# A transformer block and a mixture-of-experts block on one core: where the feed-forward stage starts, and in which order its last down products are made

## The reference, cut to what matters

```
def swiglu(x, w_gate, w_up, w_down):
    return (jax.nn.silu(x @ w_gate) * (x @ w_up)) @ w_down

# first block, around the change
f = swiglu(rms_norm(h, ffn1_norm_pre), ffn1_w_gate, ffn1_w_up, ffn1_w_down)
h = h + 0.5 * rms_norm(f, ffn1_norm_post)
u = rms_norm(h, mix_norm_pre)
proj = u @ w_in                 # queries, keys, values, recurrence, gates
...
f = swiglu(rms_norm(h, ffn2_norm_pre), ffn2_w_gate, ffn2_w_up, ffn2_w_down)
h = h + 0.5 * rms_norm(f, ffn2_norm_post)

# second block: the modulation, computed from c and w_ada
mod = jax.nn.silu(c) @ w_ada + b_ada
```

## Time and profile before

| | |
|---|---|
| time, median of 3 runs | 2217.12 us (2217.07 to 2219.19) |
| profiled execution, its own time | 2215.6 us |
| its span | 2213.7 us, granted clock 0.99 |
| PE busy | 2145.5 us, 97% |
| PEld busy | 1317.0 us, 59% |
| DVE busy | 853.4 us, 39% |
| ACT busy | 379.9 us, 17% |
| moved by the DMA engines | 581.61 MB, mean 263 GB/s |

### The profile page before, as it was taken

The page is one execution under the profiler, slowest core; times in us unless marked ns, Lnnn a source line. Parts: engine busy times, 40 slices in busy tenths (PEclk is TensorE's granted clock), DMA queues, the critical chain, the costliest instruction groups (busy, mean ns, idle before and its releaser), DMA issues.

```text
span 2213.7 us, 33878 instructions
## 1 busy us (share of the span) xinstructions
PE 2145.5 (97%) x14809; PEld 1317.0 (59%) x14810; DVE 853.4 (39%) x1400; ACT 379.9 (17%) x812; POOL 92.6 (4%) x106
## 2 busy tenths in 40 slices
PE   8999999999999999999998999999999999999997
PEld 6667687888677765678887533444444444344432
DVE  2667386621344444367777511112211121111113
ACT  1001200240111122344333110001100110000000
POOL 1000000000000011122121000000000000000000
PEclk9999999999999999999999899999999999999999
DMA  8697766244535460000012699999999999999996
GB/s 302 217 317 238 264 237 209 86 143 153 199 115 171 155 226 10 3 3 3 23 51 98 266 383 426 424 427 425 425 425 427 425 425 423 419 423 426 426 426 268
DMA packets 153876, 581.61 MB, mean 263 GB/s; under 512 B 9556, under 2 KB 108700, under 8 KB 120704
## 3 DMA queue, kind: packets, MB, share of 16 engines
q1 hardware_dynamic: 149744, 564.70, 64.9%
q0 software_dynamic: 3568, 12.72, 1.7%
q10 hardware_dynamic: 416, 2.01, 0.3%
HBM read 578.32 MB, written 3.43 MB: 263 GB/s over the span
## 4 chain that ended last, share of the span: by engine, by line
PE 90%; DVE 5%; DMA 2%; issue 1%; ACT 1%; SPq 1%; DVEq 0%
PE ps L2876 23%; PE ps L728 11%; PE ps L2884 10%; PE ps L919 8%; PE ps L796 7%; PE ps L1636 4%; PE ps L2855 3%; PE ps L2917 3%; PE ps L1079 2%; PE ps L1012 2%; PE ps L1965 2%; PE ps L1985 2%; PE ps L2067 1%; PE ps L1253 1%; DMA arena<-in_w 1%; PE ps L1982 1%
## 5 line engine op out<-in xcount | busy, mean ns | idle before, releaser
L2876 PE MATMUL ps<-ring,const 128*64 128x512 f32 (+1 forms) x1536 | 473.9, 596 | 0.0
L2876 PEld LDWEIGHTS ps<-ring,const 128*64 128x64 f32 (+1 forms) x1536 | 160.6, 144 | 304.8 <-issue 304.5
L2876 PE MATMUL ps<-arena,const 128*64 128x512 f32 (+1 forms) x512 | 225.7, 593 | 0.0
L3115 DVE TENSOR_SCALAR arena<-ps 128x1024 f32<-128x1024 f32 x18 | 22.0, 1225 | 469.3 <-PE ps L2876 469.3
L2884 PE MATMUL ps<-ring,const 128*64 128x512 f32 (+1 forms) x768 | 190.4, 594 | 1.0 <-DMA ring<-in_w 1.0
L728 PE MATMUL ps<-ring,arena 128*128 128x256 f32 x800 | 185.0, 382 | 4.6 <-DMA ring<-in_ffn_w_down 4.4
L919 PE MATMUL ps<-arena,ring 128*128 128x256 f32 x800 | 173.0, 379 | 0.0
L728 PEld LDWEIGHTS ps<-ring,arena 128*128 128x128 f32 x800 | 151.2, 191 | 26.4 <-issue 4.4
L919 PEld LDWEIGHTS ps<-arena,ring 128*128 128x128 f32 x800 | 152.0, 190 | 20.9
L796 PE MATMUL ps<-ring,arena 128*128 128x512 f32 x352 | 154.7, 592 | 0.0
L2884 PEld LDWEIGHTS ps<-ring,const 128*64 128x64 f32 (+1 forms) x768 | 65.6, 143 | 112.4 <-issue 110.9
(11 more groups left out here) (517 smaller groups left out, 2604.0 us busy)
## 6 DMA issues: line engine op xcount, KB each, us to landing
ring<-in_w SPq DMA_DIRECT2D x96, 2048.0 KB, 19.4
ring<-in_w SPq DMA_DIRECT2D x96, 1024.0 KB, 17.2
arena<-in_w SPq DMA_DIRECT2D x32, 2048.0 KB, 20.1
ring<-in_w_in SPq DMA_DIRECT2D x26, 1536.0 KB, 7.3
arena<-in_w SPq DMA_DIRECT2D x32, 1024.0 KB, 19.2
ring<-in_w_ada SPq DMA_DIRECT2D x16, 1536.0 KB, 7.7
ring<-in_ffn_w_gate SPq DMA_DIRECT2D x44, 512.0 KB, 4.9
ring<-in_ffn_w_up SPq DMA_DIRECT2D x44, 512.0 KB, 6.1
```

What stands on the lines that cost most here:

```text
L2876: ins = pe.matmul(ps[a * n:(a + 1) * n, q, :], xsT[:, k, a * n:(a + 1) * n], chunk(chunks[a])[:, q * 512:(q + 1) * 512], start=False, stop ...
```

## The change

Five edits. Ten products of the identity with itself go to PSUM bank 6, which nobody reads before it is written anew; they stand on PE behind the turned input and ahead of the first block. In the opening of `f1` the two groups of products of tile 1 that need only slot 0 (`first_rows`) stand ahead of the wait for slot 1; in `f2` they stay where they were. `hidT` has three buffers in place of two, and `hid1` and `gate8` move by 512 columns to make room. In chunk 9 (`FC - 2`) too, only tile 0's down products of the chunk before are made; those of tile 1 for chunks 8, 9 and 10 all stand behind the last turn, with chunk 8's first half of the columns ahead of `post_y` in the place of chunk 9's.

```diff
--- before.py
+++ after.py
@@ -123,6 +123,7 @@
     return i - ADA_LATE + 1 if i >= ADA_LATE else ADA - ADA_LATE + 2 * (i + 1)
 
 
+UNREAD = 10
 IN2_TILES = (3, 3, 3, 3, 2, 2, 2, 2)
 
 
@@ -380,7 +381,7 @@
 
         uT, post, first, base, up1, up0, hid0, xn, diag = area(
             arena, [[P, KD, S], [P, D], [P, S], [P, S], [P, S], [P, S], [P, S], [P, TT, D], [P, TT, P]], 0, AW)
-        hidT, hid1 = area(arena, [[P, 2, 2 * S], [P, S]], 7168, 8448)
+        hidT, hid1 = area(arena, [[P, 3, 2 * S], [P, S]], 7168, 8960)
         hids = (hid0, hid1)
         unread = [area(arena, [[P, 512]], lo)[0] for lo in (3840, 6656, 4352)]
         mixes, sums = {}, {}
@@ -411,7 +412,7 @@
         hT2, = area(arena, [[P, KD, 2 * S]], 9216)
         ln0g, ln0b = area(arena, [[P, D], [P, D]], 6400)
         ctxt = xn
-        gate8, = area(arena, [[KD, 2, P]], 8448, 9216)
+        gate8, = area(arena, [[KD, 2, P]], 8960, 9216)
         w2d, a2i, g2g, w0b, a0b, kkb, kab, gngb, gnbb, rkb, modT, cmu, shifted, fold, fold1, fold_pairs = area(
             arena, [[P, RW], [P, RW], [P, 2, RW], [P, 2, RW], [P, 2, RW], [P, RW], [P, RW], [P, RW], [P, RW],
                     [P, 2, RW], [P, 48, 2], [P, 3, 16], [P, 2, 2 * S], [P, 2, 2, 8], [P, 2, 8], [P, 2, 8]], 13312, AW)
@@ -732,18 +733,24 @@
         def ffn_up_opening_pe(pe, tag):
 
             gate_lo, up_lo, gate_hi, up_hi = weights(tag, 0)
+
+            def first_rows():
+                pe.wait_ge(*at("uT", nth(PRES, tag, 3, 3)))
+                ffn_product(pe, 1, 0, tokens_of(1, 0), gate_lo, True)
+                ffn_product(pe, 1, 1, tokens_of(1, 0), up_lo, False)
             pe.wait_ge(*at("uT", nth(PRES, tag, 3, 2)))
             landed(pe, ffn_slot(tag, 0))
             ffn_product(pe, 0, 0, tokens_of(0, 0), gate_lo, True)
             ffn_product(pe, 0, 1, tokens_of(0, 0), up_lo, False)
             if tag == "f2":
                 raw_turn_pe(pe, tag, 1)
+            else:
+                first_rows()
             landed(pe, ffn_slot(tag, 1))
             ffn_product(pe, 0, 0, tokens_of(0, 1), gate_hi, False)
             ffn_product(pe, 0, 1, tokens_of(0, 1), up_hi, False).then_inc(*up("ffn_pe"))
-            pe.wait_ge(*at("uT", nth(PRES, tag, 3, 3)))
-            ffn_product(pe, 1, 0, tokens_of(1, 0), gate_lo, True)
-            ffn_product(pe, 1, 1, tokens_of(1, 0), up_lo, False)
+            if tag == "f2":
+                first_rows()
             last_quarter(pe, tag)
             ffn_product(pe, 1, 0, tokens_of(1, 1), gate_hi, False)
             ffn_product(pe, 1, 1, tokens_of(1, 1), up_hi, False).then_inc(*up("ffn_pe"))
@@ -793,7 +800,7 @@
                 s = slot(ffn_slot(tag, 2 * c + f))
                 for tt in tiles:
                     for nh in parts:
-                        ins = pe.matmul(ps[:, 4 + 2 * tt + nh, :], hidT[:, c % 2, f * S + tt * P:f * S + (tt + 1) * P],
+                        ins = pe.matmul(ps[:, 4 + 2 * tt + nh, :], hidT[:, c % 3, f * S + tt * P:f * S + (tt + 1) * P],
                                         s[:, 2048 + nh * 512:2048 + (nh + 1) * 512], start=(c == 0 and f == 0), stop=(c == FC - 1 and f == 1))
                 if tiles[-1] == 1 and parts[-1] == 1:
                     ins.then_inc(*up("w_used"))
@@ -806,16 +813,17 @@
                     ffn_up_opening_pe(pe, tag)
                 else:
                     (ffn_up_plain_pe if c < PLAIN[tag] else ffn_up_pe)(pe, tag, c)
-                if c == FC - 1:
+                if c >= FC - 2:
                     ffn_down_pe(pe, tag, c - 1, (0,))
                 elif c:
                     ffn_down_pe(pe, tag, c - 1)
                 beside(c)
                 ffn_turn_pe(pe, tag, c)
-            ffn_down_pe(pe, tag, FC - 2, (1,), (0,))
+            ffn_down_pe(pe, tag, FC - 3, (1,), (0,))
             ffn_down_pe(pe, tag, FC - 1, (0,)).then_inc(*up("post_y"))
-            ffn_down_pe(pe, tag, FC - 2, (1,), (1,))
-            ffn_down_pe(pe, tag, FC - 1, (1,))
+            ffn_down_pe(pe, tag, FC - 3, (1,), (1,))
+            for c in (FC - 2, FC - 1):
+                ffn_down_pe(pe, tag, c, (1,))
 
         factors = [stat[:, 54 + tt:55 + tt] for tt in range(TT)]
 
@@ -837,7 +845,7 @@
                     a.activation(hid1, hid1, ACT.Silu, scale=factors[1]).then_inc(*up("ffn_act"))
                 beside(c)
                 ffn_wait(a, "ffn_pe", tag, c, "turned")
-                a.activation(hidT[:, c % 2, :], ps[:, 1, :], ACT.Copy).then_inc(*up("ffn_act"))
+                a.activation(hidT[:, c % 3, :], ps[:, 1, :], ACT.Copy).then_inc(*up("ffn_act"))
 
         def ffn_sums_dve(d, tag):
 
@@ -3363,6 +3371,8 @@
             setup_pe(pe)
             for tt in range(TT):
                 raw_turn_pe(pe, "f1", tt)
+            for _ in range(UNREAD):
+                pe.matmul(ps[:, 6, 0:P], ident, ident, start=True, stop=True)
             ffn_pe(pe, "f1", lambda c: setup_end_pe(pe) if c == 1 else bias_pe(pe, c - 2))
             pe.wait_ge(*at("const_rest", 16))
             qkv_pe(pe)
```

## The result

The changed kernel takes 2229.80 us (median of 5 runs, 2228.00 to 2231.29), the kernel before 2217.12 us (5 runs, 2216.29 to 2220.41): 12.7 us more, ratio 1.0053, interval 1.0042 to 1.0065. It is slower, by 2.5 us more than the 10.2 forecast and inside the range. The profiled execution took 2230.11 us, its span is 2228.3.

A forecast was written before the change was run, and what follows sets the result against it. TensorE (PE), busy 97% of the span, bounds the kernel. Opening -2.9, late load +11.4, clock +0.5, second block +1.2 give +10.2 us on the profiled 2215.6: 2225.8, or 2227.3 as median; range 2223.5 to 2232.5.

The forecast's parts named there:

- The opening: Start of the first block: 16 instructions fill the wait for slot 1, ten products keep the clock up; gain 2.9 us.
- The rival in which the ten run slowly and stand in the way: Opening: ten products at half clock put 1.8 us before the first product; 2229 to 2230, within the main case's 0.79.
- The waits in chunk 10: First block's end: PE waits 1.1 us for mixed weights and 1.2 for `base`, leaving 1.05 of 3.45 us.
- The load and DVE's queue: First block's end: `ada` 15 loads late, its sum blocks DVE's queue ahead of the next stage's input; loss 11.4 us.
- The third rival: Line 1024: moved products also cover PE's 2.7 us idle, no wait for mixes; -5.6 us, 2211.5, chance 0.03.
- The clock: Behind the long idle at line 1024: a further slow stretch of PE costs 0.5 us, between 0 and 1.7.
- The second block: Its end: PE waits 1.1 us for mixed weights, no `ada` slot; loss 1.2 us, 0 if slack is left.
- The sum: Whole kernel: -2.9 + 11.4 + 0.5 + 1.2 = +10.2 us, median 2227.3; main case's chance 0.79.

The follow-up runs named there:

- Moving the one call: Whole changed kernel, with DVE's sum of `ada` slot 15 moved from ahead of between_dve to behind it: 2216.77 us, 0.9997 of before.
- the last run: Whole change, `ada` 15 summed behind between_dve, tile 0's root (ACT), diagonal and outputs (DVE) ahead of tile 1's squares and gain: 2212.61 us, 0.9984 of before.
- the run with the same order and without the moved products: Opening's edits, old down products' order, tile 0's root (ACT) and diagonal and outputs (DVE) ahead of tile 1's squares and gain: 2210.58 us, 0.9969 of before.
- PE kept busy: Whole changed kernel plus 48 unread products on PE behind the first block's last down product: 2225.35 us, 1.0039 of before.

## Why the prediction was right, and where it was off

**The opening.** Forecast 2.9, measured 3.12. That the ten products keep the clock up, and that PE runs past slot 1's landing without a stop, is as it was put; without the ten, 0.6 of the gain is left, less than the 1.2 reckoned from one execution, since the clock can be low there from the start. Two small readings were off without effect: the low clock of the earlier trace rows began at 12.8 and not 12.9, and of the 4.4 us of waits for weights only 0.9 stood later in the block, the rest in the opening; the 0.9 and the 2.9 were kept, as put. The rival in which the ten run slowly and stand in the way appeared in part in one run (below), with 0.7 us and not 1.8.

**The waits in chunk 10.** Forecast 1.1 and 1.2, 2.3 together; measured 0.95 and 1.00 as idle time, 2.5 by the starts of the rows. PE's last 32 instructions began 4.0 earlier, of which the opening is 3.1: 0.9 is what the eight moved products (3.45) were worth there, forecast 1.05.

**The load and DVE's queue.** Release forecast at 236.85 - 2.9 = 233.95, measured 233.90; landing in 6.9, measured 7.0; loss at line 1024 forecast 11.4, measured 8.34 + 3.12 = 11.46. Moving the one call takes PE's wait from 11.63 to 2.71. The third rival (the moved products cover the wait for the diagonal) failed at the place given, DVE's order. With that changed, in the last run, they cover what is left of it, 0.5 and not 2.7, and the kernel is not faster for them: the run with the same order and without the moved products is the faster one by 2.0.

**The clock.** This term was mis-sized: 0.5, with 1.7 as its bound, and it measured 10.69 - 8.34 = 2.35. I took a further slow stretch like that of the opening, 3.4 us. After 11.6 us of idle it lasted some 17 us. Nine of them lay behind PE's new start (in the kernel before 3.4, from 244.9 to 248.3), over PE's work in two pieces with a wait between. The nearest row was no upper bound for a longer idle.

**The second block.** Forecast 1.2, measured 11.88 - 10.69 = 1.19, with the wait foreseen (0.95 as idle time, 1.2 by the starts of the rows); the run with that edit alone shows the same 1.2.

**The sum.** Forecast +10.2. Up to the second block's end the traces show 11.88; the 1.7 too little is the clock's 1.85, less 0.2 of the opening. The medians differ by 12.7. Between the profiled executions another 2.6 us arise in the recurrent mixer, in short waits (line 1993, 1985 before, put down to issue: 1.6 us in place of 0.2; line 1973 for DVE's line 2357: 2.0 in place of 0.3). From the second group of transposes to its end the trace of before takes 1388.9 us. Seven of the eight experiments' traces take 1.2 to 3.6 us longer, also those that come there 2.5 to 7 us earlier, but that of the opening alone takes 0.4 less; the execution of before that was profiled was 1.5 below its median. So I take the 2.6 for the luck of single executions and not for the change; that is argued, not shown, and what sets these waits was not tried.

## What to carry to other kernels

An edit that keeps a ring slot longer delays the load that reuses it, and what counts is not whether the load's data are urgent but what stands behind the first instruction that waits for it, in that engine's queue. Look for that instruction before moving a release. Before products are moved to cover a wait, ask whether the thing waited for is made in time at all: here the order on DVE and ACT was worth some 3 us, without moving a single product. And a PE that must wait can lose again afterwards through its clock: 2.35 us behind the wait of 11.6, on top of what the wait of 2.7 had cost. Products that nobody reads held the clock in both places tried, as long as they ended before the data landed; where they ended late, they cost 0.7.

## What the runs showed of the hardware

The same idle of 2.7 us ahead of line 1024 brought the clock down in some executions and not in others: the 16 instructions behind it took 3.65 us before and 3.58 with the opening alone, but 2.02 in the run with `ada` 15 summed later and in the one with the second block's new order. The wait of 2.91 us for mixed weights in chunk 6 does the same: the 16 behind it took 5.41 us before and in the changed kernel, 3.72 in three of the runs (the opening without the ten, `ada` 15 later, PE kept busy; there a wait of 1.0 for `base` follows and takes much of it back), and 6.72 in one. The ten products took between 2.40 and 3.60 us, by the moment at which the clock rose; in the longest case the first weights' products began at 12.29, 0.7 late. So a single profile carries 1 to 2 us of chance at each such place.

Whether transposes alone bring the clock up differs too. In the kernel before nothing but the 16 transposes and a small product went ahead, and six of the first weights' instructions ran in the microsecond after 12.0, so the clock had come up. In the last run (`ada` 15 later, other order) it rose while the transposes still ran, and the ten products were at full rate from their start:

```profile
5.55 3.41 PE L591 MATMUL ps<-const,h 128*128 128x128 f32 x16
8.80 2.40 PE L3376 MATMUL ps<-const 128*128 128x128 f32 x20
```

In the run without the ten products it was still low after the same transposes, and stayed so until 17; with the down products' order only, until 15. The Trainium skill, "TensorE: Matmul & The Clock Gate", part 4, says that transposes don't bring up the clock. That the trace disagrees with it, as the prediction has it, holds for these two executions and not in general.
